# Id lists without gates: what changes ahead of the expert products of a hybrid decoder step

## The reference, cut to what matters

```
scores = sigmoid(xt @ w_router);  biased = scores + router_bias
# the group with the largest sum of its two best; the two best experts inside it
gates = top_s / top_s.sum(-1, keepdims=True)
comb = (one_hot(top_idx, N_EXPERTS) * gates[..., None]).sum(1)
for e in range(N_EXPERTS):
    h = silu(xt @ w_gate[e]) * (xt @ w_up[e])
    out = out + comb[:, e:e + 1] * (h @ w_down[e])
x = layer_norm(ALPHA * x1 + out)
```

## Time and profile before

| | us |
|---|---|
| Median of 3 runs | 1299.25 (1299.21 to 1302.53) |
| Profiled execution, its own time | 1302.82 |
| Span of that execution | 1301.2 |
| TensorE busy | 1213.3 (93%) |
| VectorE busy | 901.8 (69%) |
| ScalarE busy | 533.4 (41%) |
| GpSimd busy | 483.9 (37%) |
| Mean granted TensorE clock over the span | 0.972 |

### The profile page before, as it was taken

The page is one execution under the profiler, slowest core; times in us unless marked ns, Lnnn a source line. Parts: engine busy times, 40 slices in busy tenths (PEclk is TensorE's granted clock), DMA queues, the critical chain, the costliest instruction groups (busy, mean ns, idle before and its releaser), DMA issues. The chain is left out here.

```text
span 1301.2 us, 24203 instructions
## 1 busy us (share of the span) xinstructions
PE 1213.3 (93%) x7245; PEld 1011.6 (78%) x7246; DVE 901.8 (69%) x1917; ACT 533.4 (41%) x881; POOL 483.9 (37%) x584
## 2 busy tenths in 40 slices
PE   7999999999878888999999688999999999999976
PEld 7997999978767755788887587888888888887852
DVE  3464886558868656557678567777787777777767
ACT  4131111111002346122333125666666666666656
POOL 3007880100031110623232033545555555455446
PEclk9999999999979989999999879999999999999988
DMA  8689593584436764246679565989889879756496
GB/s 246 192 316 290 181 267 123 170 265 167 160 106 211 216 223 120 100 155 240 236 265 300 200 259 210 293 266 322 262 270 327 257 230 294 196 155 169 107 296 254
DMA packets 141303, 290.08 MB, mean 223 GB/s; under 512 B 54634, under 2 KB 71610, under 8 KB 129940
## 3 DMA queue, kind: packets, MB, share of 16 engines
q1 hardware_dynamic: 122868, 225.70, 49.9%
q0 software_dynamic: 17328, 61.41, 19.2%
q10 hardware_dynamic: 1040, 2.10, 0.4%
HBM read 177.90 MB, written 111.13 MB: 222 GB/s over the span
## 5 line engine op out<-in xcount | busy, mean ns | idle before, releaser
L2407 DVE TENSOR_TENSOR wgu<-w_raw,wgu (+1 forms) x192 | 229.9, 1220 | 89.0 <-ACT wgu L2510 88.7
L2673 PE MATMUL p_gu<-wgu,xg_high 128*128 x768 | 244.4, 399 | 9.2 <-issue 4.6
L2510 ACT CAST wgu<-w_raw x188 | 192.7, 1052 | 62.2 <-issue 62.0
L2673 PEld LDWEIGHTS p_gu<-wgu,xg_high 128*128 128x128 f32 x768 | 139.7, 189 | 43.7 <-issue 17.3
L2673 PE MATMUL p_gu<-wgu,xg_low 128*128 x384 | 150.7, 392 | 0.0
L2272 POOL TENSOR_TENSOR spare_e<-nothing 128x1 f32<-128x1 f32 x48 | 46.5, 969 | 217.2 <-DVE yo L2426 217.2
L2273 POOL DMA_INDIRECT acc_rows<-yo,si x48 | 112.3, 2339 | 8.7 <-issue 8.5
L1995 PE MATMUL p_out<-w_out_high,mixt_high 128*128 128x512 f32 x256 | 102.3, 400 | 0.0
L1995 PE MATMUL p_out<-w_out_low,mixt_high 128*128 128x512 f32 x256 | 100.6, 393 | 0.0
L1995 PE MATMUL p_out<-w_out_high,mixt_low 128*128 128x512 f32 x256 | 100.6, 393 | 0.0
L2673 PEld LDWEIGHTS p_gu<-wgu,xg_low 128*128 128x128 f32 x384 | 72.1, 188 | 15.5
(11 more groups left out here) (521 smaller groups left out, 2951.0 us busy)
## 6 DMA issues: line engine op xcount, KB each, us to landing
w_raw<-in_w_gate SPq DMA_DIRECT2D x16, 1024.0 KB, 7.3
w_raw<-in_w_up SPq DMA_DIRECT2D x16, 1024.0 KB, 9.9
wd_high<-w_down_high SPq DMA_DIRECT2D x16, 1024.0 KB, 6.7
wd_low<-w_down_low SPq DMA_DIRECT2D x16, 1024.0 KB, 9.0
ya_u<-in_w_down SPq DMA_DIRECT2D x38, 256.0 KB, 4.8
w_down_low<-ya_r SPq DMA_DIRECT2D x38, 256.0 KB, 5.7
acc_rows<-ax SPq DMA_DIRECT2D x18, 512.0 KB, 6.8
xin<-in_x_prompt SPq DMA_DIRECT2D x16, 512.0 KB, 5.3
```

The lines of the kernel that those rows point to most:

```text
L2407: low = tt(wgu[:, slot, 1, at], raw[:, slot, at], wgu[:, slot, 0, at].bitcast(F32), ALU.subtract)
L2510: nc.scalar.copy(wgu[:, slot, 0, at], raw[:, slot, at]).then_inc(hi_set, 1)
L2673: mm = t.matmul(pg[b][:, :, :], x[:, b, k, :], w[h][:, k], start=(k == 0 and x is xh and h == 0), stop=(k == KD - 1 and x is xl))
```

## The change

- **Gates.** They are no longer part of the lists. In the router phase GpSimd combines masks and gates into `comb` (`combine`), 16 numbers for each token, with the experts in order of rank; the store puts them behind the `x1` row, so that rows of `x1_dram` are 1040 wide. A gather brings them along, and `hidden` reads its one number from the gathered row at a place that comes from a new row of `tab` (row 5). The last six tiles are combined and stored at the start of the expert phase, ahead of SP's first weight load; the gathers wait for these stores. A slot of `xg` is now free only when `hidden` is through with it, so a gather also waits for that (`h_set`).
- **Counts.** GpSimd also keeps a running sum `cum` of the masks. TensorE's two count products become nine, all into one bank of PSUM, and give the sums over earlier tiles ready made.
- **Places.** VectorE's 21 instructions become 11; tile and row come by rounding in f32 instead of by shifts of integers.
- **Tables.** `rowhot` now holds the id instead of 1. VectorE makes it tile by tile with a two-operation scalar instruction (all 17 tiles of the first choice, 3 of the second), ScalarE the other 14 as a Square and a Relu. Values are chosen so that the Relu gives the id on a match and 0 otherwise. `hot` is used as it is, in f32r, 48 wide; there is no `tilehot`. Each of the 34 products waits for its own table piece.
- **Idle products.** 18 and 26 instead of 48 and 32.
- **ScalarE's order.** Its tables come ahead of its first weight pieces, and a Silu on one column stands behind these.
- **w_down.** SP issues the first two experts' `w_down` only when the first gather has landed.
- **Registers.** VectorE loads two register values at the start of a step instead of one.
- **Small things.** GpSimd's loop in the router phase is written out, a few constants go and come, `b_both` lies elsewhere, and SP waits for `h_set` before it loads the last norm's rows.

```diff
-        x1_dram = dram("x1_rows", [SEQ + NS, D])
+        XW = D + E
+        x1_dram = dram("x1_rows", [SEQ + NS, XW])
...
+            def combine(gp, ch, lo, n):
+                at = slice(lo, lo + n)
+                for k, one in enumerate((oh1, oh2)):
+                    ch.mark(gp.tensor_tensor(part_k[:, k, 0:n], one[:, at, :], gate_k[:, k, at].unsqueeze(2).broadcast_to([P, n, E]), ALU.mult))
+                ch.settle()
+                by_rank = comb[:, at, :].rearrange("p t (j g) -> p t g j", g=EG)
+                return gp.tensor_tensor(by_rank, *(part_k[:, k, 0:n].rearrange("p t (g j) -> p t g j", g=EG) for k in range(2)), ALU.add)
...
+                def count(step):
+                    lo, n = CHOICES[step]
+                    gp.wait_ge(chosen, list(CHOICES).index(step) + 1)
+                    combine(gp, ch, lo, n).then_inc(comb_set, 1)
+                    for t in range(lo, lo + n):
+                        ch(gp.tensor_tensor(cum[:, t + 1], cum[:, t].bitcast(F32), msk[:, t].bitcast(F32), ALU.add))
...
+                sp.wait_ge(comb_set, 1)
+                sp.dma_start(x1_dram[LAST * P:SEQ, D:].rearrange("(t p) e -> p t e", p=P), comb[:, LAST:CH, :]).then_inc(comb_in, 16)
+                sp.dma_start(x1_dram[SEQ:, D:], comb[0:NS, CH, :]).then_inc(comb_in, 16)
                 for e in range(2):
                     gate_up(e)
                 for e in range(2):
+                    raw_landed(e)
+                sp.wait_ge(xg_in[0], 16)
+                for e in range(2):
                     down(e)
-                for e in range(2):
-                    raw_landed(e)
                 sp.wait_ge(prep_done, 1)
...
                         gp.wait_ge(x_turned, i - GS + 1)
+                        gp.wait_ge(h_set, i - GS + 1)
...
+                pre = pd[0][:, 0:TILES * E].rearrange("p (t e) -> p t e", e=E)
+                cnt = pd[0][:, TILES * E:(TILES + 1) * E].rearrange("p (g j) -> p j g", g=EG)
+                ch(ts(nt[:].rearrange(by_rank, g=EG), cnt, HALF_TILE, 1.0 / P, ALU.add, ALU.mult))
+                ch(ts(nt[:], nt[:], ROUND, None, ALU.add))
+                ch(ts(nt[:], nt[:], -ROUND, 1.0, ALU.add, ALU.max))
                 ch(v.tensor_tensor_scan(te[:], ones_e[:], nt[:], 0.0, ALU.mult, ALU.add))
+                ch(stt(first[:].rearrange("p (g j) -> p j g", g=EG), te[:].rearrange(by_rank, g=EG), -HALF_TILE / P,
+                       nt[:].rearrange(by_rank, g=EG), ALU.add, ALU.subtract))
+                ch(stt(pos[:], first[:].unsqueeze(1).broadcast_to([P, TILES, E]), float(P), pre, ALU.mult, ALU.add))
+                ch(tt(mine[:], oh12[:], pos[:].unsqueeze(1).broadcast_to([P, 2, TILES, E]), ALU.mult))
+                ch(rd(red[:], mine[:], axis=AX, op=ALU.add))
+                ch(ts(tilef[:], red[:], 1.0 / P, ROUND, ALU.mult, ALU.add))
+                ch(ts(tilef[:], tilef[:], -ROUND, None, ALU.add))
+                stt(rowf[:], tilef[:], -float(P), red[:], ALU.mult, ALU.add).then_inc(rowf_set, 1)
...
+                    for c in range(k * ROW_ACT, TILES):
+                        ts(rowhot[:, k, c], i128[:], rowf[:, k, c:c + 1], id1[:, c:c + 1], ALU.is_equal, ALU.mult).then_inc(row_set, 1)
...
+                ts(g_idx[:], p_ls[:, :], -1.0, 0.0, ALU.add, ALU.max).then_inc(lists_set, 1)
...
-                    v.scalar_tensor_tensor(hh[:, b, :], pg[b][:, 1, :], gates[:, bass.ds(i, 1)], sl[:, b, :], ALU.mult,
+                    v.scalar_tensor_tensor(hh[:, b, :], pg[b][:, 1, :], xg_all[:, bass.ds(at, 1)], sl[:, b, :], ALU.mult,
...
+                    at = dve.value_load(tab[0:1, 5, bass.ds(i, 1)], min_val=D, max_val=GS * XW - 1)
...
+                act.wait_ge(rowf_set, 1)
+                for c in range(ROW_ACT):
+                    if c >= 2:
+                        act.wait_ge(row_act, c - 1)
+                    nc.scalar.activation(apart[:, c % 2, :], i128[:], ACT.Square, bias=rowf[:, 1, c:c + 1], scale=-1.0).then_inc(apart_set, 1)
+                    act.wait_ge(apart_set, c + 1)
+                    nc.scalar.activation(rowhot[:, 1, c], apart[:, c % 2, :], ACT.Relu, bias=id1[:, c:c + 1],
+                                         scale=minus_id[:, c:c + 1]).then_inc(row_act, 1)
                 act.wait_ge(raw_ready, 1)
                 high(1)
...
+                nc.scalar.activation(warm[:], id1[:, 0:1], ACT.Silu)
...
+                t.matmul(pd[0][:, 0:(TILES + 1) * E], below[:], flat, start=True, stop=False)
+                t.matmul(pd[0][:, 0:LAST * E], ones2[:], cum[:, 0:LAST].rearrange("p t e -> p (t e)"), start=False, stop=False)
+                rest = pd[0][:, 0:(TILES + 1) * E].rearrange("p (t e) -> p t e", e=E)
+                n = TILES + 1 - LAST
+                t.matmul(rest[:, LAST:], ones2[:], cum[:, LAST:LAST + 1].broadcast_to([P, n, E]), start=False, stop=False)
+                for c in range(LAST, TILES):
+                    n = TILES - c
+                    mm = t.matmul(rest[:, c + 1:], ones2[:], msk[:, c:c + 1].broadcast_to([P, n, E]), start=False, stop=(c == TILES - 1))
+                mm.then_inc(cnt_prod, 1)
...
-                idle_products(48)
+                idle_products(18)
                 for k in range(2):
-                    pe.wait_ge(row_set, k + 1)
-                    pe.wait_ge(ids_put, (1, 3)[k])
-                    pe.wait_ge(gates_put, (TILES, TILES + BY_ACT)[k])
+                    pe.wait_ge(hot_set, k + 1)
                     for c in range(TILES):
-                        mm = t.matmul(p_ls[:, :, :].rearrange("p a b -> p (a b)"), rowhot[:, k, c, :],
-                                      tilehot[:, k, c].rearrange("p a b -> p (a b)"), start=(k == 0 and c == 0),
-                                      stop=(k == 1 and c == TILES - 1))
+                        if k and c < ROW_ACT:
+                            pe.wait_ge(row_act, c + 1)
+                        else:
+                            pe.wait_ge(row_set, k * (TILES - ROW_ACT) + c + 1)
+                        mm = t.matmul(p_ls[:, :], rowhot[:, k, c], hot[:, k, c], start=(k + c == 0), stop=(k == 1 and c == TILES - 1))
```

More of the change, by code:

```diff
@@ L1580, in hybrid_step @@
         assert late_ones.at <= base
-        reset = sb("reset", [P, E, TILES], where=steady)
-        ones_f = sb("ones_f", [P, P], where=steady)
+        CHOICES = {6: (0, 4), 10: (4, 4), 13: (8, 3)}
+        LAST = sum(n for _, n in CHOICES.values())
+        comb = sb("comb", [P, TILES, E], where=steady)
+        cum = sb("cum", [P, LAST + 1, E], F32R, where=steady)
+        ones_f = sb("ones_f", [P, P], where=Place(nc, late.at))
         assert steady.at <= mixs_at + 2 * WA * 4
@@ new lines, in _ @@
+                gp.wait_ge(sel_set, 9)
+                def count(step):
[4 more added lines that the diff above has]
+                        ch(gp.tensor_tensor(cum[:, t + 1], cum[:, t].bitcast(F32), msk[:, t].bitcast(F32), ALU.add))
+                for p in range(2, CH - 2):
+                    low(p + 2, p % 2)
+                    root(p, p % 2)
+                    if p - 2 in CHOICES:
+                        count(p - 2)
@@ L1787, in _ @@
                 low(CH, 0)
-                for p in range(CH - 2, CH + 1):
-                    root(p, p % 2)
+                root(CH - 2, 0)
+                root(CH - 1, 1)
+                count(CH - 3)
+                root(CH, 0)
             @block.scalar
@@ L2071, in tmp @@
                 return sb(name, shape, dt, where=pt)
[L2073 to L2078 removed]
+            pos, mine = tmp("pos", [P, TILES, E]), tmp("mine", [P, 2, TILES, E])
+            red, rowf, tilef = (tmp(n, [P, 2, TILES]) for n in ("red", "rowf", "tilef"))
+            first = tmp("first", [P, E])
+            nt, te = tmp("nt", [P, E]), sb("te", [P, E], where=late)
             past, of_tile, tix, tsl = tmp("past", [P, E]), tmp("of_tile", [P, 2]), tmp("tix", [1, NT]), tmp("tsl", [1, NT])
             lst, pad = tmp("lst", [P, NT]), tmp("pad", [P, NT])
[L2081 removed]
+            hot = tmp("hot", [P, 2, TILES, NT], F32R)
+            apart = tmp("apart", [P, 2, P])
+            warm = tmp("warm", [P, 1])
             assert pt.at <= base + 35 * KB, pt.at - base
[L2083 to L2084 removed]
+            rowhot = sb("rowhot", [P, 2, TILES, P], F32R, where=Place(nc, base + 35 * KB))
             g_idx, s_idx = sb("g_idx", [P, NT], U32, where=late), sb("s_idx", [P, NT], U32, where=late)
[L2086 to L2087 removed]
+            small = Place(nc, base + 51 * KB + 512)
+            tab = sb("tab", [P, 6, NT], I32, where=small)
             tab_r = sb("tab_r", [P, 2], I32, where=small)
@@ L2129, in hybrid_step @@
             assert rows.at <= zi_at + EARLY * D * 4
-            b_both = sb("b_both", [2, D], where=Place(nc, base + 47 * KB))
+            b_both = sb("b_both", [2, D], where=Place(nc, zi_at + 3 * D * 4))
+            assert rows.at <= zi_at + 3 * D * 4
             def row_of(c):
@@ L2408, in prep, with hidden @@
```

(6 more changed lines are left out.)

144 lines of the change are left out of this document (51 added, 93 removed).

## The result

The changed kernel took 1304.49 us (median of 20 executions, 1297.74 to 1308.11), the kernel before 1299.23 beside it: ratio 1.003 [1.0018, 1.0043]. Taken again as experiment e4 it gave 1302.4 us, 1.0022 [1.0004, 1.0039].

What follows compares the result with a forecast made beforehand. TensorE was taken to bound the kernel from 790 to 1250 us, with no model arithmetic in the bridge before it. The first gate/up product 8.8 us earlier took 1299.25 to 1290.4 us; range 1284.5 to 1297.

Steps and rivals of the forecast that it cites:

- "Nothing" for the stages before: Before the experts: added GpSimd work and gate stores lie beside a running TensorE and cost nothing.
- The loop, "hidden": Experts' loop: VectorE's extra register load and gate read hide in its waits for ScalarE, 1.7 us each; cost nothing.
- Rival D: Loop: register load and gate read exposed in each of 48 steps, a loss from 1.9 us on; 1309 us; chance 0.07.
- Clock behind the spin: Idle products behind the list: half clock for 13.4 of 26, full for the rest; spin ends at 777.2.
- The bridge: Router to first expert product: first gate/up product at 780.7 instead of 789.54, 8.8 us earlier.
- Counts: Start of the bridge: nine count products instead of two cost 0.5 us more, bounds 0.3 to 2.0.
- VectorE's chain: Bridge, from VectorE's first instruction to the row numbers: 3.83 us instead of 7.93.
- ScalarE's tile: Bridge tables: each Square and Relu pair takes 0.80 us, fourteen 11.2 us, setting the end of the list.
- w_down behind the gather: Moving these loads behind the first gather costs nothing and spares the gather sharing the DMA engines with them.
- Rival B: Bridge: ScalarE's tile takes 0.55 us, or the clock stays up through the list; 11.5 to 12.4 us off; chance 0.20.
- C: Rival: loads moved behind the gather land late, ScalarE stands 9 us, 6 us lost; 1296 us; chance 0.12.
- E: Rival: late counts (2.0), a split gather and a stalled ScalarE eat the gain; within 0.3%; chance 0.05.

Runs made afterwards that it cites:

- e4: The changed kernel as it is, measured again: 1302.4 us, ratio 1.0022 to the kernel before.
- e1: The kernel before with 131,584 unused bytes added behind the x1 rows in DRAM, nothing else changed: 1308.22 us, ratio 1.0056.
- e2: The kernel before with 135,168 unused bytes added behind the x1 rows, which gave the same addresses as e1: 1307.47 us, ratio 1.0056.
- f2: The kernel before with only the accumulator moved, by 135,168 bytes; w_down scratch stays in place: 1299.59 us, ratio 1.0005.
- h1: The kernel before with one more, unused register load by VectorE in every step of the experts' loop: 1303.07 us, ratio 1.0018.
- g3: The kernel of e3 with the first two experts' w_down loads issued in the old order, ahead of the first gather: 1298.67 us, ratio 0.9992.
- e3: The changed kernel with 56 unused rows added to its x1 table, moving the tensors behind it: 1295.23 us, ratio 0.9971.
- f1: The kernel before with 364,544 unused bytes behind its x1 rows, so w_down scratch and accumulator stand as in e3: 1302.55 us, ratio 1.0022.
- f3: The changed kernel with its x1 table declared last, so w_down scratch and accumulator stand where they stood before: 1298.42 us, ratio 0.9988.
- k1: The kernel of e3 with 10 ScalarE tables, 18 idle products behind the list, and GpSimd, not VectorE, fetching gates, two tiles ahead: 1291.43 us, ratio 0.9941.

## Why the prediction failed, step by step

- **"Nothing" for the stages before.** This step failed, and it decides the sign. It weighed the longer row as a packet and the gate stores as instructions, and those cost nothing, but not that a longer tensor moves all that is declared behind it. In the profile 5.2 us were lost there, all of it in phase 1. By medians the price is higher: e1 and e2 are 8.1 and 7.4 us above before (1300.09 beside them), against a forecast gain of 8.8. No rival had it.
- **The loop, "hidden".** Failed in size: 2 to 3 us, not 0. The argument was an average (1.7 us of wait for ScalarE a step); the load stands ahead of a chain that the next steps' weights hang on, and VectorE's idle time there went down to 0.6 us in single steps of before, which the mean hides. Rival D named this mechanism, with a decision point at 1.9 us and 1309 us; its price was far too high, its sign right. The prediction's test, "wrong if the loop is longer than before by over 1 us", fired.
- **Clock behind the spin.** It was forecast to be full again after 13.4 idle products and to stay. It did come back inside the spin, but did not stay: 0.57 from 786 to 790 us. That cost 1.3 us here, and up to 3 us in others (18.5 to 18.7 in the column "to down"). Such late clocks also occur with before's bridge (f2, h1), so this is a term of spread as much as of the change.
- **The bridge.** Right: 8.1 us of 8.8, with the spin as the last wait, though two misses offset each other. The list was ready 18.5 us behind the first count product, drawn at 16.9, and the spin took 8.0 us, drawn at 8.8. By its own sign (last list product within 1 us of 768, here 5.2 later) the list was late. Counts took 2.1 us from the first product to VectorE, before 0.8: +1.3 for 0.5 (six products of at most 96 columns take 1.40 us). The bound of 1.9 us in that step is worked out from eight short products, where it says seven. VectorE's chain 3.7 us for 3.83. ScalarE's tile 0.82 for 0.80, in order, and it set the end of the list. Gather 4.2 for 4.2.
- **w_down behind the gather.** "Cost nothing": right. "The gather would share the engines with that load": no; with the old order (g3) the bridge is 30.7 us, the same.
- **Rival B** (0.55 us a tile, or full clock) is false by ScalarE's rows, and by the granted clock of 0.50 from 775 to 779 us. **C**: no wait of TensorE for w_raw or w_down stands among the waits of after. **E** had the right outcome at the low end, by causes that did not occur; late counts were +1.3, not 2.0, and the gather was not split: the software queue has 17328 packets before and after. So the rule of the Trainium skill's "DMA: Bandwidth & Descriptors" (SWDGE vs HWDGE vs iDMA), that a packet is preferably at most 4096 bytes, priced nothing here for rows of 4160.

With places equal, what is the change worth? By medians -7.3 us (e3 against f1), -5.4 (e4 against the mean of e1 and e2), -1.4 (f3 against before, with x1_rows elsewhere). By the traces -8 for the bridge, +0 to +3 for the clock, +2 for the loop: about -4.

What stays open: why the place costs at all, and why 33 pages cost more than 48 and 89; whether the high or the low w_down scratch does it; why f1 is 2.8 us above before; and why shorter bridges stall the loop more as long as the register is on VectorE (10.2 and 12.7 us), which k1's 7.1 only circumscribes.

## What to carry to other kernels

When a change alters the size of a DRAM scratch tensor, compare the start of the first changed instruction before anything else; if code ahead of it is late in several profiles, pad the tensor until the addresses agree in both kernels, and only then judge the change. A wait that is long on average does not hide an instruction put ahead of a chain; run it dead in the old kernel and see. An in-order queue that takes over a small job must do it early enough that the wait ahead of it in the queue is not the one its reader hangs on.

## What the runs showed of the hardware that was not expected

- DRAM places: with the tensors behind x1_rows 135,168 bytes further on, the last product of phase 1 started at 258.8 to 261.9 us; at 0, 196,608 and 364,544 bytes at 252.5 to 258.0. Between 110 and 125 us ScalarE waited 4.6 to 5.2 us for a load at 135,168 bytes, 3.4 to 3.9 at 364,544, 3.0 at 196,608 and 1.6 to 2.5 at 0. For equal bytes (225 GB/s over 255 us) the DMA engines' busy share was 0.75 to 0.76 at 135,168 and 0.73 to 0.75 elsewhere.
- A register load on VectorE in each step of the loop cost 2 to 3 us in all. The runs with it on VectorE show 5 to 13 waits of "issue" of 1.4 to 2.8 us ahead of a step's first weight piece, most of them in every second step; of the eight others one (f1) shows a single one of 0.5 us.
- Nine f32r products of 288 to 16 columns at half clock hold VectorE up for 2.1 us. The last six, of 96 down to 16 columns, start 0.20 to 0.22 us apart whatever their length; their weight loads have the same distance. The list products of 48 columns start 0.11 us apart where the clock is full (from 764.2 us).
